# Inverting the delta rule's triangular matrix: how often the narrow products come between the wide ones

## The reference, cut to what matters

```python
lmat = jnp.where(strict, jnp.einsum("bhnid,bhnjd->bhnij", k_beta, k) * decay, 0.0)
amat = lmat + jnp.eye(c, dtype=jnp.float32)
rhs = jnp.concatenate([v * beta[..., None], k_beta * jnp.exp(g)[..., None]], axis=-1)
sol = lax.linalg.triangular_solve(amat, rhs, left_side=True, lower=True, unit_diagonal=True)
u, w = sol[..., :dv], sol[..., dv:]
```

## Time and profile before

| | us |
|---|---|
| median of 3 runs | 2287.73 (2286.22 to 2289.42) |
| the profiled execution | 2288.66 |
| its span, first to last instruction | 2286.1 |
| TensorE busy in the span | 2250.3 (98%) |
| VectorE busy | 1061.1 (46%) |
| GpSimd busy | 1689.8 (74%) |
| ScalarE busy | 1089.1 (48%) |

### The profile page before, as it was taken

How to read it: one execution, slowest core, us unless ns; L and a number is a source line. 1 busy time by engine, 2 the same in 40 slices (tenths; PEclk the granted TensorE clock), 3 DMA queues, 4 the chain that set the end, 5 groups by cost and what they waited for, 6 DMA issues and landing times.

```text
span 2286.1 us, 41578 instructions
## 1 busy us (share of the span) xinstructions
PE 2250.3 (98%) x16571; PEld 2053.6 (90%) x16571; DVE 1061.1 (46%) x1918; ACT 1089.1 (48%) x1317; POOL 1689.8 (74%) x1337
## 2 busy tenths in 40 slices
PE   9999999999999999999999999999999999999998
PEld 8888999999988888899999998889898888898887
DVE  4334755324233333465553233334435765534766
ACT  5335444465433533464444734336655335565333
POOL 6997855556899899975554678996567997655996
PEclk9999999999999999999999999999999999999999
DMA  7554533334565555544333445565334556333553
GB/s 253 191 194 154 160 112 118 114 115 137 166 201 186 182 185 197 188 153 125 111 117 107 136 160 184 183 213 147 105 120 146 199 186 179 126 112 123 195 196 121
DMA packets 316572, 359.96 MB, mean 157 GB/s; under 512 B 20820, under 2 KB 295312, under 8 KB 316304
## 3 DMA queue, kind: packets, MB, share of 16 engines
q1 hardware_dynamic: 316074, 357.65, 48.5%
q10 hardware_dynamic: 358, 0.33, 0.0%
HBM read 356.91 MB, written 1.05 MB: 157 GB/s over the span
## 4 chain that ended last, share of the span: by engine, by line
PE 95%; DVE 2%; ACT 1%; POOL 1%; issue 0%; DMA 0%; SPq 0%; ACTq 0%; DVEq 0%
PE ps L800 26%; PE ps L611 22%; PE ps L643 17%; PE ps L648 9%; PE ps L677 4%; PE ps L930 1%; PE ps L912 1%; PE ps L1204 1%; PE ps L693 1%; PE ps L1256 1%; POOL sb_lo L576 1%; PE ps L933 1%; PE ps L664 1%; PE ps L1227 1%; PE ps L839 1%; PE ps L1087 1%
## 5 line engine op out<-in xcount | busy, mean ns | idle before, releaser
L576 POOL TENSOR_TENSOR sb_lo<-sb_raw,sb_hi 128x512 fp32r<-128x512 f32 x1333 | 1689.6, 1302 | 578.7 <-ACT sb_hi L1363 577.5
L1363 ACT ACTIVATE sb_hi<-sb_raw 128x2048 fp32r<-128x2048 f32 (+2 forms) x341 | 639.1, 1876 | 748.5 <-PE ps L648 358.3
L643 PE MATMUL ps<-sb_hT,sb_hi 128*128 128x512 f32 x1792 | 426.0, 390 | 0.0
L643 PEld LDWEIGHTS ps<-sb_hT,sb_hi 128*128 128x128 f32 x1792 | 332.7, 188 | 66.6
L800 PE MATMUL ps<-sb_hT,sb_hi 128*128 128x256 f32 x2304 | 310.0, 287 | 2.8 <-DVE sb_hT L2224 2.8
L800 PEld LDWEIGHTS ps<-sb_hT,sb_hi 128*128 128x128 f32 x2304 | 285.1, 191 | 9.0 <-DVE sb_hT L2224 3.2
L648 PEld LDWEIGHTS ps<-sb_hT,sb_lo 128*128 128x128 f32 x1792 | 229.8, 191 | 8.7
L1966 DVE TENSOR_TENSOR sb_yinv<-ps,sb_row 128x512 f32<-128x512 f32 x112 | 77.5, 692 | 337.2 <-PE ps L648 336.4
L648 PE MATMUL ps<-sb_hT,sb_lo 128*128 128x256 f32 x1792 | 232.4, 283 | 0.0
L611 PE MATMUL ps<-sb_hi,sb_o_h 128*128 128x512 f32 x560 | 219.8, 392 | 0.4 <-DVE sb_o_l L1973 0.4
L611 PE MATMUL ps<-sb_hi,sb_o_l 128*128 128x512 f32 x560 | 218.6, 390 | 0.0
(11 more groups left out here) (403 smaller groups left out, 3336.9 us busy)
## 6 DMA issues: line engine op xcount, KB each, us to landing
sb_raw<-in_ffn_w_in SPq DMA_DIRECT2D x87, 1024.0 KB, 5.1
sb_raw<-in_w_in SPq DMA_DIRECT2D x76, 1024.0 KB, 5.3
sb_raw<-in_ffn_w_out SPq DMA_DIRECT2D x44, 1024.0 KB, 4.9
sb_raw<-in_ffn_w_up SPq DMA_DIRECT2D x44, 1024.0 KB, 5.1
sb_raw<-in_ffn_w_down SPq DMA_DIRECT2D x22, 1024.0 KB, 5.0
sb_raw<-in_w_out SPq DMA_DIRECT2D x16, 1024.0 KB, 5.2
sb_raw<-in_w_branch_a SPq DMA_DIRECT2D x8, 1024.0 KB, 5.1
sb_raw<-in_w_branch_b SPq DMA_DIRECT2D x8, 1024.0 KB, 5.1
```

The source lines that it names most:

```text
L576: ins = nc.gpsimd.tensor_tensor(lo[:, slot, c], raw[:, slot, c], hi[:, slot, c].bitcast(F32), ALU.subtract)
L643: mm(ps[:, bank + i, :].rearrange("p (h n) -> p h n", h=2), wh[:, c, i * P:(i + 1) * P], hT_both[:, :, c, :], start=c == 0, stop=False, sk ...
L1363: fn(hi[:, slot, 0:width], raw[:, slot, 0:width], ACT.Copy).then_inc(hi_ready, 1)
```

## The change

The product M = L Y is no longer computed anew on each level. It is kept in PSUM (bank 2) and updated as the inverse is: with E = -mask * M, M += M E, X += E^T X, and T += E^T T, where T is the transpose of M, which is the stationary operand of M's update. T lies beside X in `xinv`, so that one VectorE addition of 128x512 updates both. All products of a level now depend on E and on the state before it alone, so a level is one visit of three groups in place of two visits of one and two. The sixth level is done apart: Y is formed in PSUM as X^T + X-product (`x5`, three groups), then `y5` and `p` join the halves. The steps of a block go from 18 to 14, the visits from 13 to 9, and the parts of the wide units are planned anew over the steps; their number is as before. `eg`, the two wide matmuls of `row_of` on bank 6, stays at level 2.

```diff
...
-put(f"inv{n}", (-1.0 if n == 0 else 1.0) * ((j // (2 * s) == i // (2 * s)) & ((later // s) % 2 == 1) & ((earlier // s) % 2 == 0)).astype(np.float32).reshape(2, H, 2, H)[[0, 1], :, [0, 1]].reshape(P, H))
+put(f"inv{n}", -1.0 * ((j // (2 * s) == i // (2 * s)) & ((later // s) % 2 == 1) & ((earlier // s) % 2 == 0)).astype(np.float32).reshape(2, H, 2, H)[[0, 1], :, [0, 1]].reshape(P, H))
...
-DELTA_PE = Steps(["turned"] + sum([[f"p{i}"] + (["eg"] if i == 2 else []) + [f"q{i}"] for i in range(LEVELS)], [])
-         + ["uw", "kv0", "ws1", "o", "osum"])
+DELTA_PE = Steps(["turned", "m0", "t0"] + sum([[f"m{i + 1}"] + (["eg"] if i == 2 else []) + [f"x{i + 1}"] for i in range(LEVELS - 2)], [])
+         + ["x5", "p", "q", "uw", "kv0", "ws1", "o", "osum"])
...
-DELTA_DVE = Steps(sum([[f"p{i}", f"y{i}"] + ([f"x{i}"] if i + 1 < LEVELS else []) for i in range(LEVELS)], [])
-          + ["qdec", "s0", "v1", "osq"])
+DELTA_DVE = Steps(sum([[f"e{i}", f"x{i}"] for i in range(LEVELS - 1)], []) + ["y5", "x5", "p", "y", "qdec", "s0", "v1", "osq"])
...
-DELTA_WEIGHT = [2] + [1] * 12 + [1.3, 1, 1, 1.5, 2]
+DELTA_WEIGHT = [2, 1.5] + [1.7] * 4 + [1.5, 1.2, 1.2] + [1.3, 1, 1, 1.5, 2]
...
+m_turned = xinv[:, S:2 * S]
+steps_of = tuple(plev[:, S * i:S * (i + 1)] for i in range(2))
...
     yield
-    for i in range(LEVELS):
-        if i:
...
-                ins = mm(part(ps[:, 2, :], p, 0), block(lmat, p, 1, 0), part(y_half, p, 1), start=True, stop=True)
+    wf("yinv")
+    for p, h in halves_of:
+        ins = mm(part(ps[:, 2, :], p, h), block(lmat, p, h, h), part(y_half, p, h), start=p == 0, stop=False, skip_group_check=True)
+    ins.then_inc(dl_pe, 1)
+    wf("attn")
+    for p, h in halves_of:
+        ins = mm(part(ps[:, 5, S:2 * S], p, h), part(y_half, p, h), block(lmat, p, h, h), start=True, stop=True)
+    ins.then_inc(dl_pe, 1)
+    yield
+    for i in range(LEVELS - 2):
+        wv(f"x{i}")
+        e_half = steps_of[i % 2]
+        for p, h in halves_of:
+            ins = mm(part(ps[:, 2, :], p, h), part(m_turned, p, h), part(e_half, p, h), start=False, stop=i == LEVELS - 3, skip_group_check=True)
         ins.then_inc(dl_pe, 1)
...
             row_of(row_blocks[1], c, 6, dl_pe)
-        yield
-        wv(f"p{i}")
...
-            wf("attn")
         for p, h in halves_of:
-            if i + 1 < LEVELS or h == 0:
-                ins = mm(part(ps[:, 2, :], p, h), part(x_half, p, h), part(p_half, p, h), start=True, stop=True)
-        if i + 1 < LEVELS:
+            ins = mm(part(ps[:, 5, :], p, h), part(e_half, p, h), part(x_half, p, h), start=True, stop=True)
+        if i < LEVELS - 3:
             for p, h in halves_of:
-                ins = mm(part(ps[:, 5, :], p, h), part(p_half, p, h), part(x_half, p, h), start=True, stop=True)
+                ins = mm(part(ps[:, 5, S:2 * S], p, h), part(e_half, p, h), part(m_turned, p, h), start=True, stop=True)
         ins.then_inc(dl_pe, 1)
         yield
-    wv(f"y{LEVELS - 1}")
+    wv(f"x{LEVELS - 2}")
+    for p, h in halves_of:
+        mm(part(ps[:, 2, :], p, h), part(x_half, p, h), cc("half")[ROWS[h], :], start=p == 0, stop=False, skip_group_check=True)
+    for p, h in halves_of:
+        mm(part(ps[:, 2, :], p, h), part(x_half, p, h), part(p_half, p, h), start=False, stop=True, skip_group_check=True)
+    for p in range(4):
+        ins = mm(part(ps[:, 5, :], p, 0), part(p_half, p, 0), part(x_half, p, 0), start=True, stop=True)
+    ins.then_inc(dl_pe, 1)
+    yield
+    wv("y5")
+    for p in range(4):
+        ins = mm(part(ps[:, 2, :], p, 0), block(lmat, p, 1, 0), part(y_half, p, 1), start=True, stop=True)
+    ins.then_inc(dl_pe, 1)
+    yield
+    wv("p")
+    for p in range(4):
+        ins = mm(part(ps[:, 2, :], p, 0), part(x_half, p, 0), part(p_half, p, 0), start=True, stop=True)
+    ins.then_inc(dl_pe, 1)
+    yield
+    wv("y")
     wa("blocks")
...
         mm(blk(2, p), of(whole, p), of(u_v, p), start=True, stop=True)
...
         output_roots(c - 1)
-    for _ in range(1 + 2 * (LEVELS - 1)):
+    for _ in range(LEVELS + 1):
         yield
-    wv(f"y{LEVELS - 2}")
+    wv("y5")
     for h, rows in enumerate(ROWS):
...
                  y_half[rows, :].rearrange("p (k n) -> p k n", n=H), ACT.Copy)
...
     yield
-    for i in range(LEVELS):
-        wp(f"p{i}")
-        if i + 1 < LEVELS:
-            tt(compact(p_half), compact(ps[:, 2, 0:S]), over(cc(f"inv{i + 1}"), 4), ALU.mult).then_inc(dl_dve, 1)
+    for i in range(LEVELS - 1):
+        wp(f"m{i}")
+        tt(compact(steps_of[i % 2]), compact(ps[:, 2, 0:S]), over(cc(f"inv{i + 1}"), 4), ALU.mult).then_inc(dl_dve, 1)
+        if i == 0:
+            wp("t0")
+            V.tensor_copy(m_turned, ps[:, 5, S:2 * S]).then_inc(dl_dve, 1)
         else:
-            V.tensor_copy(p_half[0:H, :], ps[0:H, 2, 0:S]).then_inc(dl_dve, 1)
+            wp(f"x{i}")
+            n = slice(0, S if i == LEVELS - 2 else 2 * S)
+            tt(xinv[:, n], xinv[:, n], ps[:, 5, n], ALU.add).then_inc(dl_dve, 1)
         if i == 0 and c:
...
         elif i == 1 and c:
...
         yield
-        wp(f"q{i}")
-        if i + 1 < LEVELS:
...
-        yield
+    wp("x5")
+    V.tensor_copy(y_half, ps[:, 2, 0:S]).then_inc(dl_dve, 1)
+    tt(x_half[0:H, :], x_half[0:H, :], ps[0:H, 5, 0:S], ALU.add).then_inc(dl_dve, 1)
+    yield
+    wp("p")
+    V.tensor_copy(p_half[0:H, :], ps[0:H, 2, 0:S]).then_inc(dl_dve, 1)
+    yield
+    wp("q")
+    ts(four(whole[0:H, :])[:, :, H:P], compact(ps[0:H, 2, 0:S]), -1.0, None, ALU.mult).then_inc(dl_dve, 1)
+    yield
     wp("eg")
...
     tt(four(attn[:]), four(attn[:]), over(cc("chunk"), 4), ALU.mult)
```

More of the change, by code:

```diff
@@ L904, in delta @@
                     yield
-                    for i in range(LEVELS):
-                        if i:
-                            wv(f"y{i - 1}")
-                        else:
-                            wf("yinv")
-                        if i + 1 < LEVELS:
[L911 to L914, removed]
-                                ins = mm(part(ps[:, 2, :], p, 0), block(lmat, p, 1, 0), part(y_half, p, 1), start=True, stop=True)
+                    wf("yinv")
[12 more added lines that the diff above has]
+                            ins = mm(part(ps[:, 2, :], p, h), part(m_turned, p, h), part(e_half, p, h), start=False, stop=i == LEVELS - 3, skip_group_check=True)
                         ins.then_inc(dl_pe, 1)
@@ L920, in delta @@
                             row_of(row_blocks[1], c, 6, dl_pe)
-                        yield
-                        wv(f"p{i}")
-                        if i:
-                            if i + 1 < LEVELS:
-                                wv(f"x{i - 1}")
-                        else:
-                            wf("attn")
                         for p, h in halves_of:
-                            if i + 1 < LEVELS or h == 0:
-                                ins = mm(part(ps[:, 2, :], p, h), part(x_half, p, h), part(p_half, p, h), start=True, stop=True)
@@ L2152, in delta @@
                     yield
-                    for i in range(LEVELS):
-                        wp(f"p{i}")
-                        if i + 1 < LEVELS:
-                            tt(compact(p_half), compact(ps[:, 2, 0:S]), over(cc(f"inv{i + 1}"), 4), ALU.mult).then_inc(dl_dve, 1)
-                        else:
-                            V.tensor_copy(p_half[0:H, :], ps[0:H, 2, 0:S]).then_inc(dl_dve, 1)
+                    for i in range(LEVELS - 1):
[4 more added lines that the diff above has]
+                            V.tensor_copy(m_turned, ps[:, 5, S:2 * S]).then_inc(dl_dve, 1)
+                        else:
+                            wp(f"x{i}")
+                            n = slice(0, S if i == LEVELS - 2 else 2 * S)
+                            tt(xinv[:, n], xinv[:, n], ps[:, 5, n], ALU.add).then_inc(dl_dve, 1)
                         if i == 0 and c:
```

## The result

| | before | changed |
|---|---|---|
| median, us | 2287.10 (4 runs, 2286.22 to 2289.42) | 2300.59 (4 runs, 2298.63 to 2301.77) |
| ratio | | 1.0054, 95% interval 1.0042 to 1.0066 |
| profiled execution, its span | 2288.66, 2286.1 | 2298.63, 2296.8 |

A forecast was written before the change was run, and what follows sets the result against it. TensorE, busy in 98% of the span, was taken as the bound. Saving -5.7, bank waits +13.2 and clock +1.7 made +9.2 us on the median 2287.73, so 2297 us, range 2290 to 2304.

The forecast's parts named there:

- Bound: Whole kernel: TensorE, busy in 98% of the span, bounds it; only its own work and waits change the time.
- Visits and groups: Inversion on TensorE: a group costs 0.46 us, a visit 0.34; per block one group more and four visits fewer.
- `row_of`: Level 2 of each block: its two wide records between narrow groups cost one form change more, +0.25 us.
- The 5.7 us saved: Inversion in two layers: 0.91 us saved in each first block and 0.65 in each of three later blocks.
- VectorE's longer addition: After each level's visit: 128x512 takes 0.69 us, covered by at least 1.63 of wide work; cost taken as 0.
- The bank waits: Delta stages: wide units wait for VectorE to empty halves of q, k, v banks; 6.6 us a layer, 13.2 added.
- The fourth: First block: z waits behind step 5 for k's second half, with VectorE coming from two full steps; about 0.25 us.
- first rival: Delta stages: bank waits don't come, as VectorE is busy in little more than half; 2282 us, chance 0.09.
- The clock: TensorE's clock at the six new large waits: one fall taken, 1.7 us, bounds 0 and 10 us.
- the third rival: Clock falls in every one of the six waits: 2305 us, chance 0.17.

The follow-up runs named there:

- thirteen-visit run: The changed kernel's products (19 groups) put in 13 visits again, with the plan weights of the kernel before: 2293.15 us, ratio 1.0021 to the kernel before.
- run without T: The changed kernel with the third plan and `row_of` behind the three groups, updates of T left out, so computation is missing: 2270.22 us, ratio 0.9926.
- third plan: The changed kernel with the third block's 28 parts placed by hand, 16 behind the nine visits and 12 behind the later steps: 2282.90 us, ratio 0.9979.
- run with the second block's numbers: The changed kernel with the second block's parts placed by the numbers of the third block: 2327.65 us, ratio 1.0178.
- the one with VectorE's work behind: The changed kernel, plan kept, with VectorE doing a step's further work behind the emptied half instead of ahead of it: 2298.34 us, ratio 1.0036.

## Why the prediction was right

The direction, the place and the mechanism held; the time was 3.6 us above the forecast, inside its range.

- **Bound.** TensorE, with nothing but its own work and waits to read. Right: every difference above is one of visits, groups, waits or clock.
- **Visits and groups.** 0.34 a visit and 0.46 a group held in the thirteen-visit run, in the run without T (0.47) and in the rows (1.55 for three groups against 1.53). The 64 narrow records more that were forecast are there, 16635 records in all against 16571.
- **`row_of`.** The sign was right and the size short, 0.33 a place instead of 0.25. The 5.7 us saved become 5.1 by that; the run with the third plan shows 4.95.
- **VectorE's longer addition.** 0.69 us, and no visit waited for it in the changed kernel. Right with nine visits; with thirteen again it did reach a visit twice a layer.
- **The bank waits.** Predicted 2.3, 1.5 and 2.55 in a third block and 0.25 in a first; measured 2.14, 1.44, 2.45 and none. The fourth rested on a backlog of two steps worked out to a quarter microsecond, finer than its terms: k's half ended 0.20 us ahead of z. 12.1 us instead of 13.2, and this 1.1 too much hid a part of what the clock term lacked. That VectorE is idle in nearly half of the stage, the first rival's argument, counted for nothing.
- **The clock.** This is the mis-sized term: one fall of 1.7 us was taken. The profiled execution had 5.1 us of it in the delta stages and 1.7 less in the later layers. Its sum is 12.1 + 5.1 - 1.7 - 5.1 = 10.4 of 10.7 us. The median lies higher: with no more clock lost than in the third plan's runs the changed kernel would stand at 2282.9 + 12.1 = 2295, so its median carries some 5.6 us of clock beyond what the third plan's runs carry. A fall in each of the six waits, the third rival, was not seen: two of the six had one, and the median, 2.0 us above that execution, leaves room for about one more. The Trainium skill ("TensorE: Matmul & The Clock Gate", section HAM oscillation) describes an engine that waits for DMA and is throttled again each time, with gaps longer than any of these waits. Here falls came behind waits of 2.14 and 2.45 us too, and behind a part of them only.

What stays open: which waits bring a fall. In the profiled executions of the changed kernel, of the run with the second block's numbers and of the one with VectorE's work behind, three of six waits of 2.14 us had a fall at their end or behind them, six of eight of 2.45, and none of six of 1.44; nothing here controls which. Nor does every fall need a wait: in all profiled executions of the study seven more came where a delta stage begins, two of them in 240:252, with TensorE busy throughout. The kernel before and the changed one had none there in their profiled executions.

## What to carry to other kernels

Where background work is dealt out over hand-written steps, every cut in the number of steps must be checked against the resources that are freed one piece a step: here the placing of 28 parts cost 17.7 us around a saving of 5. Lay the plan out, and for each user of a buffer add up what stands ahead of its release in the releasing engine's queue; a load of 56% says nothing of it. And count changes between narrow and wide products, also those in the middle of a step, at their measured price.

## What the runs showed of the hardware

- A wait of TensorE of 1.1 to 2.5 us can cost more than its own length again by the clock, 5.2 us around one of 2.45; after others it costs nothing. One program so varies from run to run, 2292.4 to 2301.1 us.
- The clock also fell where TensorE had waited for nothing, at the start of a delta stage: 0.86 in 12 us with the engine busy for all 12.00, 1.7 us.
- Four 64x64 products on one quadrant take as long as eight on two, 0.60 and 0.61 us a visit: two quadrants work side by side.
